# Post-norm hand-overs on one core: residual and new term turned by transposing instructions, residual first, next unit waits slice by slice

## The reference, cut to what matters

```
x = x + merged @ w_out                                # q = 0
x = x + square(relu(norm(x) @ w_up)) @ w_down         # q = 1
for l in 0, 1:
    x = x + 0.5 * rms_norm(swiglu(rms_norm(x)), g)    # q = 2, 5
    x = x + rms_norm(mixer(rms_norm(x)), g)           # q = 3, 6
    x = x + 0.5 * rms_norm(swiglu(rms_norm(x)), g)    # q = 4, 7
```

## Time and profile before

| | us |
|---|---|
| timed runs | 1581.01, 1587.80, 1587.93 |
| their median | 1587.8 |
| span of the profiled execution, first to last instruction | 1579.1 |
| mean granted TensorE clock in it | 0.965 |
| PE busy in it | 1473.9 |

### The profile page before, as it was taken

The page is one execution under the profiler, slowest core; times in us unless marked ns, Lnnn a source line. Parts: engine busy times, 40 slices in busy tenths (PEclk is TensorE's granted clock), DMA queues, the critical chain, the costliest instruction groups (busy, mean ns, idle before and its releaser), DMA issues.

```text
span 1579.1 us, 25067 instructions
## 1 busy us (share of the span) xinstructions
PE 1473.9 (93%) x9970; PEld 1333.5 (84%) x9970; DVE 947.6 (60%) x1370; ACT 710.0 (45%) x1154; POOL 248.1 (16%) x213
## 2 busy tenths in 40 slices
PE   3799988879999999999999899999999998899998
PEld 3688777768998889988889799988999886799986
DVE  7998437746664466654776566645655456565644
ACT  5323024434443354443544654536445355554443
POOL 6944210000220001100410111101111010011100
PEclk9799967889999999999999999999999999999999
DMA  6333142033555545555343255554555551245551
GB/s 246 107 107 134 67 135 104 1 107 133 187 187 186 187 160 186 199 187 187 140 142 139 91 212 187 202 187 155 184 186 199 190 187 54 81 151 183 202 188 63
DMA packets 36515, 242.04 MB, mean 153 GB/s; under 512 B 4176, under 2 KB 5328, under 8 KB 8784
## 3 DMA queue, kind: packets, MB, share of 16 engines
q1 hardware_dynamic: 34560, 235.55, 41.9%
q10 hardware_dynamic: 1872, 5.33, 1.0%
HBM read 239.58 MB, written 1.05 MB: 152 GB/s over the span
## 4 chain that ended last, share of the span: by engine, by line
PE 82%; DVE 9%; ACT 4%; POOL 4%; issue 1%; DMA 1%; ACTq 0%; DVEq 0%; POOLq 0%
PE ps L1783 46%; PE ps L1823 24%; DVE wlo L988 3%; PE ps L1997 2%; PE ps L1894 2%; PE ps L1971 1%; PE ps L1846 1%; PE ps L1847 1%; ACT whi L572 1%; POOL cosT L1687 1%; PE ps L1926 1%; PE ps L1885 1%; DVE alo L1333 1%; POOL sinT L1689 1%; PE ps L1987 1%
## 5 line engine op out<-in xcount | busy, mean ns | idle before, releaser
L988 DVE TENSOR_TENSOR wlo<-raw,whi 128x1024 fp32r<-128x1024 f32 (+1 forms) x434 | 519.9, 1240 | 312.3 <-ACT whi L572 312.1
L1783 PE MATMUL ps<-ahi,whi 128*128 128x256 f32 x2112 | 597.7, 283 | 34.2 <-DVE wlo L988 20.6
L572 ACT ACTIVATE whi<-raw 128x1024 fp32r<-128x1024 f32 (+1 forms) x434 | 426.7, 1032 | 434.9 <-PE ps L1783 232.3
L1783 PE MATMUL ps<-alo,whi 128*128 128x256 f32 x2112 | 593.2, 281 | 0.0
L1783 PE MATMUL ps<-ahi,wlo 128*128 128x256 f32 x2112 | 592.3, 280 | 0.0
L1783 PEld LDWEIGHTS ps<-ahi,whi 128*128 128x128 f32 x2112 | 400.8, 190 | 43.2 <-issue 19.2
L1783 PEld LDWEIGHTS ps<-alo,whi 128*128 128x128 f32 x2112 | 400.8, 190 | 0.7 <-issue 0.7
L1783 PEld LDWEIGHTS ps<-ahi,wlo 128*128 128x128 f32 x2112 | 399.9, 189 | 0.0
L1721 POOL TENSOR_TENSOR hlo<-fh,hhi 128x256 f32 (+3 forms) x104 | 85.7, 824 | 750.5 <-ACT hhi L806 538.9
L1392 DVE TENSOR_TENSOR fa<-ps,r 128x512 f32<-128x512 f32 x104 | 71.9, 692 | 169.4 <-PE ps L1783 169.2
L1823 PE MATMUL ps<-wlo,hhi 128*128 128x512 f32 x480 | 150.7, 395 | 0.0
(11 more groups left out here) (337 smaller groups left out, 1535.9 us busy)
## 6 DMA issues: line engine op xcount, KB each, us to landing
raw<-in_w_gu SPq DMA_DIRECT2D x88, 1024.0 KB, 4.9
raw<-in_w_fd SPq DMA_DIRECT2D x44, 1024.0 KB, 4.9
raw<-in_w_up SPq DMA_DIRECT2D x16, 1024.0 KB, 4.9
raw<-in_w_dn SPq DMA_DIRECT2D x16, 1024.0 KB, 4.9
raw<-in_w_ret SPq DMA_DIRECT2D x13, 1024.0 KB, 4.9
raw<-in_w_mg SPq DMA_DIRECT2D x8, 1024.0 KB, 4.9
raw<-in_w_o SPq DMA_DIRECT2D x8, 1024.0 KB, 5.6
raw<-in_w_mem SPq DMA_DIRECT2D x4, 1024.0 KB, 4.9
```

Of the source, the lines that this page charges most:

```text
L572: nc.scalar.activation(whi[:, m % SPL, c], raw[:, n % RAW, c], ACT.Copy).then_inc(S("w_hi"), 1)
L988: ins = tt(wlo[:, m % SPL, c], raw[:, n % RAW, c], whi[:, m % SPL, c].bitcast(F32), ALU.subtract)
L1783: ins = mm(dst, lhsT, rhs, start=k == 0 and p == 0, stop=k == kt - 1 and p == len(pairs) - 1)
```

## The change

For q = 2 to 6 PE no longer makes pairs of fp32 matmuls. Both the old residual and the new term are turned with `is_transpose=True` and accumulated in PSUM; only the first of a bank has `start`. The 8 instructions of the residual of a token half are issued together, those of t = 0 before the first wait for `y_new`, those of t = 1 after the new term of t = 0. The number of instructions on PE stays at 32. For all q the signal `t_lo` is given after each slice of t = 1 and not for t = 0, and the next unit waits before each slice k.

```diff
--- before.py
+++ after.py
@@ -1332,7 +1332,8 @@
                         k, s = 4 * h + i, slice(t * P, t * P + P)
                         ins = stt(alo[:, k, s], PS[turned(t, h)][:, i * P:i * P + P], pre_gain(q)[:, k:k + 1],
                                   ahi[:, k, s].bitcast(F32), ALU.mult, ALU.subtract)
-                    ins.then_inc(S("t_lo"), 1)
+                        if t:
+                            ins.then_inc(S("t_lo"), 1)
 
                 if post:
                     dve.wait_ge(S("in_gain"), 16 * (pi + 1))
@@ -1829,24 +1830,37 @@
 
             def transposed(q):
 
-                for t in range(TT):
-                    for h in range(2):
-                        if q < FIRST_POST:
+                def old_residual(t):
+                    for k in range(KT):
+                        h, i = k // 4, k % 4
+                        mm(PS[turned(t, h)][:, i * P:i * P + P], xr[:, t, k * P:k * P + P], C["ident"], is_transpose=True,
+                           start=i == 0, stop=False, skip_group_check=True)
+
+                def new_term(t, h):
+                    pe.wait_ge(S("y_new"), 4 * (q - FIRST_POST) + 2 * t + h + 1)
+                    for i in range(4):
+                        k = 4 * h + i
+                        ins = mm(PS[turned(t, h)][:, i * P:i * P + P], yr[:, t, k * P:k * P + P], C["ident"],
+                                 is_transpose=True, start=False, stop=i == 3, skip_group_check=True)
+                    ins.then_inc(S("x_tr"), 1)
+
+                if q < FIRST_POST:
+                    for t in range(TT):
+                        for h in range(2):
                             pe.wait_ge(S("x_new"), 4 * q + 2 * t + h + 1)
-                        else:
-                            pe.wait_ge(S("y_new"), 4 * (q - FIRST_POST) + 2 * t + h + 1)
-                            if t == 0 and h == 0:
-                                pe.wait_ge(S("x_new"), 4 * q)
-                        for i in range(4):
-                            k = 4 * h + i
-                            dst = PS[turned(t, h)][:, i * P:i * P + P]
-                            if q < FIRST_POST:
-                                ins = transpose(dst, xr[:, t, k * P:k * P + P], C["ident"])
-                            else:
-                                mm(dst, xr[:, t, k * P:k * P + P], C["ident"], start=True, stop=False)
-                                ins = mm(dst, yr[:, t, k * P:k * P + P], C["ident"], start=False, stop=True)
-                        ins.then_inc(S("x_tr"), 1)
-                return lambda k: pe.wait_ge(S("t_lo"), 4 * q + 3 + k // 4) if k % 4 == 0 else None
+                            for i in range(4):
+                                k = 4 * h + i
+                                ins = transpose(PS[turned(t, h)][:, i * P:i * P + P], xr[:, t, k * P:k * P + P], C["ident"])
+                            ins.then_inc(S("x_tr"), 1)
+                else:
+                    pe.wait_ge(S("x_new"), 4 * q)
+                    old_residual(0)
+                    new_term(0, 0)
+                    new_term(0, 1)
+                    old_residual(1)
+                    new_term(1, 0)
+                    new_term(1, 1)
+                return lambda k: pe.wait_ge(S("t_lo"), 8 * q + k + 1)
 
             def token_roots(q):
                 pe.wait_ge(S("diag"), q + 1)
```

## The result

| | before | after |
|---|---|---|
| median of the timed runs, us | 1587.9 (6 runs, 1580.5 to 1590.4) | 1575.6 (6 runs, 1571.3 to 1578.6) |
| span of the profiled execution, us | 1579.1 | 1572.3 |
| mean granted clock in it | 0.965 | 0.961 |

The ratio is 0.9938, with a 95% interval of 0.9914 to 0.9963. Two later comparisons of the same pair gave 0.9926 (0.9908 to 0.9944) and 0.9925 (0.9905 to 0.9946). The change makes the kernel faster, by 10 to 12 us; the interval of the first ratio reaches from 6 to 14. A timed run is 1.75 to 1.94 us longer than its span wherever the span is listed, but for two runs of one experiment (2.6 and 2.8); the profiled execution of before therefore belongs to the timed run of 1581.0, not to the median.

A forecast was written before the change was run, and what follows sets the result against it. TensorE, busy 93% of the span, was taken to bound the kernel. Hand-over gains of 13.6 us less 2.8 for the clock gave 10.8, so 1587.8 - 10.8 = 1577.0 us, range 1568 to 1585.

The forecast's parts named there:

- Step 1, the price: Turning at q = 2 to 6: a transposing instruction costs 0.13 us, accumulating included, against 0.22 for an ordinary matmul.
- the rival: Turning at q = 2 to 6: accumulating transposes cost 0.22, PE stays pace maker, gain 8.2 us, 1579.6; chance 0.08.
- The 0.3 for the early start: Part of the 0.22-price rival's gain at each of q = 2 to 6, from starting the residual early: 0.3 us.
- 0.8 and 0.29: Same rival, each of q = 2 to 6: 0.8 us from the finer wait, 0.29 from PE's wait for the last slices.
- Step 2, the chain: Hand-over q = 2: PE ends turning 3.5 us earlier, ACT's 16 slices end at 757.5, 2.6 earlier.
- The places asked for: Profile signs: ACT's slices in one 4.2 us block from the root, DVE's behind the second `yr` pair, 32 instructions in 4.2.
- Step 3, the finer wait: Next unit's start: 2.15 us earlier at q = 2, 0.8 of it the finer wait; 0.8 alone at q = 0 and 1.
- The sum: Gain over all hand-overs without the clock: 3 x 2.4 + 2 x 2.6 + 0.8 + 0.45 = 13.6 us.
- Step 4, what is late next: Second unit's weights: 2.4 to 2.6 us earlier, 2.6 after q = 2 and 5, 0.44 at q = 1; POOL's margin 0.2.
- Step 5, the clock: Stillness behind q = 2 to 6: 1.7 falls of the granted clock at 1.7 us each, 2.8 us lost.
- The chance of 1 in 3 a hand-over: Chance given to each of q = 2 to 6 that the granted clock falls there, so 1.7 falls.
- The Trainium skill's rule on transposes and the clock: Transposes do not count as PE busy, so the clock falls at all five hand-overs; 1586.7 to 1591; chance 0.13.

The follow-up runs named there:

- the one with H = 8.36: Changed kernel with ordinary fp32 matmuls for the transposing ones; 1584.7 us, ratio 0.9980. H: us from start of `down`'s last matmul to the next unit.
- the late order: Changed kernel, q = 2 to 6, residual and new term turned slice by slice behind the `y_new` wait; 1571.0 us (0.9900), repeated 1570.3 (0.9908).
- the first experiments: The runs taking the change apart: finer wait alone 1586.0 us, old coarse wait 1583.3, residual not early 1571.0, ordinary matmuls in the new order 1584.7.
- the coarse wait: Changed kernel with the kernel before's wait and signals, so transposing and early residual alone; 1583.3 us, ratio 0.9977; 7.10 from `down` to the next unit.
- the late residual with unused matmuls: Changed kernel with residual turned slice by slice behind the wait, seven unused matmuls at q = 0 and 1, five at q = 2 to 6; 1567.4 us, 0.9872.

## Why the prediction was right

**Step 1, the price.** 0.13 was taken, 0.11 measured, and accumulating is free: the `yr` row at 749.99 takes 1.04 for eight like the `xr` row at 749.12. With 0.22 the kernel would have been the one with H = 8.36, 3.5 us below the kernel before in the median; the rival gave it 8.2. The 0.3 for the early start was about right up to the second unit (0.25), though in H it is a loss of 0.5. What the rival had wrong is the finer wait: it counted 0.8 and 0.29 in full at each of the five, which the second unit's weights do not let through.

**Step 2, the chain.** The places asked for were ACT's slices from the end of its root, DVE's right behind the second `yr` pair, and PE out of the way. All are in the timeline. The next unit was predicted 6.5 after the last matmul of `down` and came after 6.33. What I did not say is that the early issue of the residual plays no part in it; the late order gives the same H, because DVE's slices start behind its own `yr` work in both.

**Step 3, the finer wait.** 0.8 in H, as q = 0 and 1 and the pair 7.10 and 6.33 show (0.77). The sum needed it only beside faster turning, and there it is worth 0.6 to 0.8. That it is worth as much by itself, as I expected of its own experiment, was wrong: at q = 2 to 6 it gains nothing alone, since the second unit's weights bind. The waits themselves cost nothing that shows.

**Step 4, what is late next.** Right, and a little low. The five post-norm hand-overs gave 2.6 to 3.4 each up to the second unit, 14.1 in all, against 12.4 in the sum. Most of the excess is q = 5: 3.4, and 3.8 in the kernels with unused matmuls there, where I had 2.6. ACT issues three loads there before it rounds, and that kept it from rounding for 2.13 before and for 1.12 after. The longest of the three issues took 1.16, 1.07 and 1.16 in the three profiles with ordinary turning matmuls (before, finer wait alone, ordinary in the new order) and 0.45 to 0.47 in all ten with transposing ones; why is open. At q = 2 I expected the stand of q = 5 and misread the place: the stand there was 0.48 before and is 0.32 after, and the gain of 2.8 is ACT's all the same. POOL ends at 755.63 and ACT's second square starts at 756.04, a margin of 0.4 where I had 0.2. At q = 1, where no fall disturbs it (seven unused matmuls everywhere), the second unit comes after 11.00 instead of 11.47: 0.47, predicted 0.45.

**Step 5, the clock.** The term was 2.8 and it is about 5 between the two profiles, with 0.4 more inside the figure of q = 5: -1.2 at q = 0 (a shorter slow stretch than before), +1.2 at q = 1, +0.6 in retention, +4.2 in the latent mixer, +0.1 at the end. The chance of 1 in 3 a hand-over came near for q = 2 to 6 (one of five), but the place of the price was wrong. At q = 5 itself the fall costs 0.4 at most, since PE waits for weights there anyway; the dear part is in the mixer behind it, where the four profiles with a fall at q = 5 took 85.5 and the nine without took 81.3 to 82.5, but for one with 84.0. And q = 1, which I had left out of the count, fell where it had not before, although its stillness shrank.

The size came out because two terms missed in opposite ways, which is luck: 14.1 + 0.5 + 0.8 = 15.4 instead of 13.6, less 5 instead of 2.8, gives 10.4, against 10.8 predicted. With the 4.5 of the faster stretch in before, and 0.85 won ahead of q = 0's hand-over, that makes the 6.8 between the spans.

The 12.3 between the medians is not taken apart by any profile. The profiled execution of before was one of the faster ones of its kernel (1581.0, others near 1588); that of the changed kernel (1574.1) lies 1.5 under its median. Of 25 timed runs of before that stand beside the first experiments the five shortest (1579.8 to 1581.7) have a mean granted clock of 0.964 to 0.967, the eighteen from 1587.0 up 0.960 to 0.965. So the longer executions may hold falls that the profile does not show, and then the change costs less clock against them than the 5 above. That is not shown. I carried the difference of spans over to the median as if the profile stood for all executions, and that it came out within 1.5 us is luck too.

The Trainium skill's rule on transposes and the clock (TensorE: Matmul & The Clock Gate, Part 4) is not borne out as I used it in the prediction, where it meant a fall at each of the five. Behind 32 transposing instructions in 4.3 us and 1.76 us of stillness four of five hand-overs kept a granted clock of 1.00 in each of three profiles of the changed kernel; q = 5 did fall, and q = 0 and 1, behind 16 such instructions and 2.17 of stillness.

## What to carry to other kernels

When a step is made cheaper on the engine that everybody waits for, follow the others to the second thing that they do: here the finer wait alone bought nothing at the post-norm hand-overs, because the next weights came no earlier, and the cheaper turning made both pay. A price saved on TensorE turns into stillness of TensorE, and stillness can lower its clock far beyond the place where it stands; look at the granted clock behind each stand, and compare a version that fills all the stands with unused matmuls, which here took another 6 us off. An early issue that does not move the last thing waited for makes the stand longer, and what it brings has to be looked for at the next wait.

## What the runs showed of the hardware

- **Falls of the clock tend to repeat at the same places of a kernel, though not in every execution.** Three profiles of the changed kernel, on different occasions, have 0.50 behind q = 0, 1 and 5, then for 10 us in the latent mixer and at three other places, and 1.00 behind the other hand-overs, while identical instructions stand at q = 2 to 6. The two later profiles behind q = 5 and in the mixer:

```profile
1279.90:1283.10 3.20, 3.20 (x15) 3.20 (x16) 2.31 (x10) 2.38 (x6) 0.41 (x1) 0.50 1.04 431
1296.90:1307.00 10.10, 6.64 (x28) 5.88 (x29) 8.64 (x12) 5.82 (x13) 0.00 (x0) 0.50 0.32 109
```

```profile
1282.00:1285.20 3.20, 3.15 (x15) 3.19 (x16) 2.35 (x10) 2.42 (x6) 0.46 (x1) 0.50 1.03 428
1299.00:1309.10 10.10, 6.60 (x28) 5.84 (x29) 8.65 (x12) 5.86 (x13) 0.00 (x0) 0.50 0.34 111
```

But the two profiles of the late residual differ at one place of the latent mixer (first line 1.00, second 0.50), and the timed runs of the changed kernel list mean clocks from 0.957 to 0.961:

```profile
1348.40:1351.60 3.20, 3.20 (x19) 2.73 (x19) 1.12 (x2) 0.63 (x1) 0.00 (x0) 1.00 0.73 297
```

```profile
1348.40:1351.60 3.20, 3.20 (x12) 2.91 (x13) 0.53 (x2) 0.63 (x1) 0.00 (x0) 0.50 0.76 302
```

- **A shorter stillness is not always safer.** At q = 1 the clock stayed up with a stand of 2.95 in the kernel before and in the one with the coarse wait, and fell with a stand of 2.17 in all nine profiles with the finer wait in which it was not filled. The length of the stand alone does not decide; what else does was not tried.
- **The same units have two speeds at full clock.** 1008 matmuls took 118.7 to 119.0 us in most stretches and 114.4 or 114.5 in five: one of the kernel before, two of the finer wait alone and one in each profile of the late residual; 720 took 81.84 instead of 84.8 in the late residual with unused matmuls. Single first units take 5.68 or 5.89. A fast long stretch is worth 4.3 us, nearly as much as the late residual won in the median. Every one of the five profiles of kernels that turn slice by slice has at least one, and none of the eight with the residual issued first has any. What picks the speed stays open, and so does whether the late residual won by it.
